# A weight ring in SBUF that begins 16 bytes past a multiple of 64

## What is computed

```python
proj = hx @ w_in                      # likewise w_uq, w_ukv, w_out, w_up, w_down, ab_w_in, ab_w_out, pool_*
def peer(h, wq, keys, u_tab, v_tab):  # u_tab, v_tab: 16384 x 1024 each, for each of two layers
    q = h @ wq
    ...                               # two top-16 searches per head give 16 experts per head and token
    act = gelu(einsum('nd,nhkd->nhk', h, u_tab[idx]))
    return einsum('nhk,nhkd->nd', gate * act, v_tab[idx])
```

## Time and profile before

| | |
|---|---|
| three runs | 2285.16, 2287.6, 2290.14 us (median 2287.6) |
| the profiled execution | 2285.66 us, its span 2284.3 us, mean granted clock 0.993 |
| busy share of the span | PE 98%, DVE 82%, ACT 53%, POOL 7% |
| DMA moved | 442.32 MB, 194 GB/s on average |

### The profile page before, as it was taken

One profiled execution on the slowest core, in us unless ns is written; L12 is line 12 of the kernel. 1 busy time (PEld: TensorE's weight loads), 2 busy tenths in 40 slices (PEclk: granted clock), 3 DMA queues, 4 the chain that ended last, 5 costly groups with the idle time before them and its releaser, 6 DMA issues.

```text
span 2284.3 us, 34778 instructions
## 1 busy us (share of the span) xinstructions
PE 2233.5 (98%) x13446; PEld 1889.3 (83%) x13446; DVE 1864.8 (82%) x3365; ACT 1201.4 (53%) x1754; POOL 168.5 (7%) x75
## 2 busy tenths in 40 slices
PE   9999999999999999999999999999999999999997
PEld 7789978777788888888887877788888888888886
DVE  8679996568689988888888888869998888887656
ACT  7555554466456555554444445455665554444553
POOL 0000000000044400000000000014430000000000
PEclk9999999999999999999999999999999999999999
DMA  8366593233556655555558996455655555556664
GB/s 292 125 203 217 196 355 117 93 120 102 184 176 185 191 177 170 172 174 175 171 176 306 340 352 233 148 185 186 189 187 169 175 172 171 175 175 223 219 234 136
DMA packets 123508, 442.32 MB, mean 194 GB/s; under 512 B 13760, under 2 KB 16832, under 8 KB 122704
## 3 DMA queue, kind: packets, MB, share of 16 engines
q1 hardware_dynamic: 117464, 425.04, 56.3%
q10 hardware_dynamic: 5880, 15.06, 1.9%
HBM read 436.88 MB, written 3.16 MB: 193 GB/s over the span
## 4 chain that ended last, share of the span: by engine, by line
PE 82%; DVE 10%; ACT 3%; DMA 3%; issue 2%; SPq 0%; ACTq 0%; DVEq 0%
PE psum L447 21%; PE psum L457 13%; PE psum L459 13%; PE psum L458 13%; PE psum L451 12%; PE psum L452 3%; PE psum L2863 3%; DVE low L2607 3%; DVE acc L1784 2%; DMA ring<-in_peer_v 2%; DVE cv L2115 1%; ACT spl L1104 1%; ACT cv L1405 1%; PE psum L925 1%; PE psum L2806 1%
## 5 line engine op out<-in xcount | busy, mean ns | idle before, releaser
L2607 DVE TENSOR_TENSOR low<-ring,spl 128x1024 fp32r<-128x1024 f32 x638 | 778.7, 1228 | 259.3 <-ACT spl L1104 258.8
L1104 ACT ACTIVATE spl<-ring 128x1024 fp32r<-128x1024 f32 x702 | 735.2, 1054 | 281.7 <-DMA ring<-in_peer_u 155.3
L447 PE MATMUL psum<-hT,spl 128*128 128x512 f32 x2016 | 520.0, 397 | 2.5 <-ACT yy_abo L1454 1.4
L447 PEld LDWEIGHTS psum<-hT,spl 128*128 128x128 f32 x2016 | 375.5, 189 | 76.7 <-DVE hT L2454 3.6
L457 PE MATMUL psum<-spl,Ws 128*128 128x512 f32 x1024 | 407.1, 398 | 6.9 <-DVE Ws L2645 6.8
L459 PE MATMUL psum<-spl,Ws 128*128 128x512 f32 x1024 | 399.5, 390 | 0.0
L458 PE MATMUL psum<-low,Ws 128*128 128x512 f32 x1024 | 398.4, 389 | 0.0
L451 PEld LDWEIGHTS psum<-hT,low 128*128 128x128 f32 x2304 | 315.7, 191 | 22.6
L451 PE MATMUL psum<-hT,low 128*128 128x256 f32 x2304 | 322.5, 283 | 0.0
L1713 ACT ACTIVATE Ws<-S 128x256 fp32r<-128x256 f32 x256 | 106.6, 417 | 354.5 <-PE psum L459 349.8
L2920 POOL TENSOR_TENSOR low<-ring,spl 128x1024 fp32r<-128x1024 f32 x64 | 162.1, 2534 | 1133.5 <-ACT spl L1104 1133.5
(11 more groups left out here) (411 smaller groups left out, 2900.1 us busy)
## 6 DMA issues: line engine op xcount, KB each, us to landing
ring<-in_peer_u SPq DMA_DIRECT2D x256, 512.0 KB, 3.5
ring<-in_peer_v SPq DMA_DIRECT2D x256, 512.0 KB, 3.6
vring<-in_ada_w SPq DMA_DIRECT2D x56, 512.0 KB, 6.1
ring<-in_w_up SPq DMA_DIRECT2D x44, 512.0 KB, 5.0
aring<-in_ada_w SPq DMA_DIRECT2D x40, 512.0 KB, 4.9
ring<-in_ab_in SPq DMA_DIRECT2D x32, 512.0 KB, 3.5
ring<-in_peer_wq SPq DMA_DIRECT2D x32, 512.0 KB, 3.8
ring<-in_w_down SPq DMA_DIRECT2D x22, 512.0 KB, 5.9
```

What stands on the lines that cost most here:

```text
L447: q.matmul(wide, w(hi, k), P.hT[:, :, k, :], start=k == 0, stop=False)
L1104: q.activation(P.spl[:, m % SLOTS, 0:w], P.ring[:, m % SLOTS, 0:w], ACT.Copy).then_inc(*P.hi.mark(m))
L2607: q.tensor_tensor(P.low[:, n % SLOTS, 0:w], P.ring[:, n % SLOTS, 0:w], P.spl[:, n % SLOTS, 0:w].bitcast(F32), ALU.subtract).then_inc(*P.lo ...
```

## The change

`ring` and `low` become tensors with 32 words more, and are used from their word 4 on: the five tiles begin at byte 16528 = 258 x 64 + 16. Each tile is still 4096 bytes, so all five slots are 16 bytes past a multiple of 64. `spl` and everything behind it lie 128 bytes higher than before, with the same remainder by 64 and by 128. The distance from a tile in `ring` to its tile in `spl` grows from 20480 to 20592 bytes. The instructions, their order on each engine, their waits and the DMAs are the same ones, with other addresses; apart from the line numbers, which are one higher behind the edit, the two programs list alike on every engine.

```diff
         low = self.base + 4 * self.at_word
-        self.ring = f("ring", [128, SLOTS, 1024])
-        self.low = nc.alloc_sbuf_tensor_at("low", [128, SLOTS, 1024], F32R, offset=low)
+        tiles = lambda t: t[:, 4:4 + SLOTS * 1024].rearrange("p (s w) -> p s w", s=SLOTS)
+        self.ring = tiles(f("ring", [128, SLOTS * 1024 + 32]))
+        self.low = tiles(nc.alloc_sbuf_tensor_at("low", [128, SLOTS * 1024 + 32], F32R, offset=low))
         self.spl = f("spl", [128, SLOTS, 1024], F32R)
```

## The result

The kernel became slower by 0.9%: 2306.8 us, the median of four runs from 2304.65 to 2309.74, against 2287.45 us of four runs before (2285.16 to 2290.14). The ratio is 1.0086, with a 95% interval from 1.0073 to 1.0098. That is 19.4 us. It lies inside the range of the prediction and outside its likeliest case, which was no change.

A forecast was written before the change was run, and what follows sets the result against it. PE was taken as the bound, with 82% of the chain. To 2285.66 us profiled it added 0 (PE), 0.6 (DVE, ACT) and 0 (DMA), giving 2286.3; the forecast was 2287 us, no change, range 2278 to 2345 us.

The forecast's parts named there:

- PE's reads of `low`: Matmuls reading the moved `low` tiles, about 4,000 of 13,446: 0 taken, upper end 4 ns each, 16 us.
- What is new is the address of three accesses: Premise: only DMA's ring write, ACT's and DVE's `ring` reads with the `low` write, and PE's `low` reads change address.
- DVE and ACT: Splitting of ring tiles: an odd start costs 5 to 10 ns per instruction, 0.6 us in the chain, lower end 0.
- The DMA's writes: Writes into `ring` at 16 past 64: not dearer, 0 us; upper end twice the time for a row.
- Rival 1: Ring rows at 16 past 32 dearer for DMA engines: slower, 2330 us at 50% more, up to 2550 if doubled; chance 0.24.
- Rival 2: PE reads `low` more slowly: 4 us per ns and matmul, 2303 us at 4 ns; 0.10, plus 0.03 for DVE or ACT.
- Rival 3: Faster: transfers of tensors moved 128 bytes, `ada_w` included, quicken in the full DMA stretches; 2279 us at 30% off; chance 0.08.

The follow-up runs named there:

- `e1_pad_only`: Changed kernel with `ring` and `low` back at a multiple of 64, the 32 words behind them kept: 2307.55 us, ratio 1.0086.
- `e5_all_up_128`: Kernel before with every tensor, ring included, 128 bytes higher, all distances kept: 2286.02 us, ratio 0.9999.
- `e7_ws_up_128`: Kernel before with only `Ws`, and the small `Eb` behind it, 128 bytes higher: 2301.21 us, ratio 1.0058.
- `e15_pad64_only`: Changed kernel with `ring` and `low` back in their places and a pad of 64 words, 256 bytes, behind them: 2287.48 us, ratio 1.0.
- `e16_all_up_32`: Kernel before with every tensor, ring included, 32 bytes higher, all distances kept: 2288.01 us, ratio 1.0008.
- `e14_all_16`: Kernel before with every SBUF tensor 16 bytes higher, all distances kept: 2294.51 us, ratio 1.0033.
- `e9_pad_after_spl`: Kernel before with 32 words put behind `spl`; `ring`, `low` and `spl` stay, everything behind moves up 128 bytes: 2310.56 us, ratio 1.0104.

## Why the prediction was wrong

**The step that failed is "PE's reads of `low`".** It was taken as 0, with 4 ns on some 4,000 matmuls, 16 us, as the upper end. Two things were wrong in it. The first is its premise, "What is new is the address of three accesses". The pad made something else new: the distances between operands. The prediction used the 128 bytes only for a possible gain in `ada_w`'s transfers. `e1_pad_only`, `e5_all_up_128`, `e7_ws_up_128` and `e15_pad64_only` together show that distances modulo 256 bytes are what costs. The second is the row it rested on. The products with `mkT` are plain fp32, with 256 columns. What was compared there was a start at 32 bytes past 64, and that indeed costs nothing (`e16_all_up_32`). It says nothing of fp32r products with 512 columns. The 4 ns themselves were put down to rounding. In the nanoseconds of the packed trace the `mkT` products start 218 to 219 apart and the pooling ones 215 to 216, so 3 ns of it are real. By the table of `Plan`, `mkT` lies 160 bytes (by 256) from `mqT`, and `pm` and `pp` a multiple of 256 apart; whether this or the 96 partitions makes the 3 ns, no run separates.

**The size.** The terms read from the groups by form of both kernels: `Ws` products 16.1 us; the other products with 512 moving columns from weight tiles (with `hT`, `aT`, `cR`, `MT`) 6.8 us; the up stage of the feed-forward part, with 256 columns, -4.0 us; the u tables, 842.5 and 842.6 us, nothing. The sum is 18.9 us. That it is near the 19.4 between the medians is luck: these rows come from the two profiled executions, between which PE's whole busy time grew by 23.5 us, and the other 4.6 us lie in smaller groups (1.4 of them in the transposes of `xr`, 9.1 to 10.5 us). The -4.0 us are busy time and no time won, since PE starts a tile of the up stage every 3.19 us before and every 3.20 after, and waits longer in between. By place, 15.9 of the 24.1 us lie in the v tables, as above. The u tables hold most of the products with `low` and lose nothing; so the prediction's price of 4 us per ns, over all `low` products, counted the wrong 4,000.

**DVE and ACT.** Right: 0.6 us was forecast; `low` went from 1229 to 1228 ns and `spl` stayed at 1054. This holds with all tensors 16 bytes higher (`e14_all_16`). POOL's splits, which the prediction had not priced, take 2534 ns before and 2523 after.

**The DMA's writes.** Right, at 0. The ring's rows at 16 bytes past 64 cost 49 us per MB as before; in the same stretch `e14_all_16` has 51, and the kernels with aligned rows lie between 47 and 52. Rival 1 is thus wrong in all its forms. The read-modify-write that the Trainium skill ("Collectives: The Full Stack", Rules for kernel authors) gives as the reason for 32-byte alignment left nothing that can be seen in these transfers; the page speaks of collectives' buffers, and no run here has one.

**Rival 2** had the right engine and, by luck, nearly the right time (2303 us at 4 ns), and the wrong mechanism. Its mark was to be starts of `low` products further apart than those of `spl`. The starts of both moved apart alike, as 1107.10, 1107.34 and 1107.57 on the timeline show. It would have made padding harmless, and padding alone is the loss.

**Rival 3** is wrong. The full stretches moved somewhat fewer GB/s (326 for 340 and 346 for 357), DMA stands in the chain for 3% as before, and with everything 128 bytes higher (`e5_all_up_128`) nothing is gained.

**What stays open.** Why the hardware wants the distance is not shown; the runs give a period, not a cause. The u tables are spared in the changed kernel because `spl` and `hT` kept their distance: where it changes (`e9_pad_after_spl`), their products with 512 columns lose 6.6 us. Not shown is why the products with 256 columns lose next to nothing, 283 to 284 ns at most (`e1_pad_only`). Why the products of `spl` with `Ws`, whose own distance is still a multiple of 256 in the changed kernel, slow down beside those of `low` is open as well. That matmuls which follow each other disturb one another would fit, but no run isolates it; a change of the distance from `low` to `spl` alone cannot be made, since one of the two then also moves against `Ws`. (With that distance kept, `e7_ws_up_128` and `e9_pad_after_spl` have the loss in full, so it is not needed for it.) Why the first tile of a pair runs at 230 ns with all distances at a multiple of 256 is open too. In the changed kernel the 16 bytes and the distance of 112 come together, and the costs don't add (`e1_pad_only` 1.0086, `e14_all_16` 1.0033, both together 1.0086), so their shares in it are not known.

## What to carry to other kernels

Keep the two operands of fp32r matmuls with 512 columns at the same remainder modulo 256 bytes, and at multiples of 32: pad by 256 bytes at a time, and round up a small tensor that stands between large ones. With 256 columns they lost 1 ns at most (283 to 284 in the u tables of `e1_pad_only`). A pad is an edit of every tensor behind it, so list the distances that it changes along with the addresses. When PE is the bound, compare the starts of its matmuls one after another on the timeline: 6 ns of 227 on some of them was most of 0.9% of this kernel, and no wait shows it.

## What the runs showed of the hardware that was not expected

- In the second tile of each pair in the v tables, where the weight tile is the moving operand, fp32r matmuls of 512 columns start every 227 ns when stationary and moving operand lie a multiple of 256 bytes apart, and every 233 to 234 ns at 16, 32, 64, 96, 128, 288 and 320 bytes. At 192 bytes it is 230 (2.76 us for twelve). In the first tile it is 230 and 233 ns, before and after.
- In the u tables, where the weight tile is the stationary operand, a distance of 128 bytes costs the products with 512 columns 3 ns each (397 to 400, `e9_pad_after_spl`), and those with 256 columns nothing (283 and 282).
- With all distances kept, a start at 16 bytes past a multiple of 32 costs 3 ns per product in the second tile of a v pair, nothing in the first, and gives back 2 ns per product of 256 columns in the u tables. In the changed kernel a tile of the up stage, from the first to the last start of its 24 products of 256 columns, went from 2848 to 2792 ns (median), for a reason that the runs don't show; `e14_all_16` has 2822. The next tile starts no sooner for it.
- DMA writes, DVE's reads and writes and ACT's reads at 16 past 64 cost what aligned ones do: 49 to 51 us per MB against 47 to 52, 1227 to 1229 ns and 1054 ns.
